# A hybrid decoder step in float32 on one Trainium2 core: sixteen places for the samples' value weights, new tokens' values over 128 rows, first modulation weights over eight places, one mixed block later

## What is computed

```
def modulated_prenorm(x, c, w_ada, b_ada, g_pre):
    mod = (jax.nn.silu(c) @ w_ada + b_ada)[:, None, :]
    shift, scale, gate = jnp.split(mod, 3, axis=-1)
    return rms_norm(x, g_pre) * (1 + scale) + shift, gate

def short_conv_mixer(h, conv_buf, w_in, w_conv, w_out):
    b_g, c_g, v, z = jnp.split(h @ w_in, 4, axis=-1)
    ...

def sample_latent_attention(q_lat, q_pe, ckv_new, kpe_new, cache_ckv, cache_kpe, page_table):
    ...
    p = jax.nn.softmax(jnp.concatenate([s_past, s_new], axis=-1), axis=-1).astype(ckv_new.dtype)
    return (jnp.einsum('bhqk,bkc->bqhc', p[..., :n_past], past_ckv)
            + jnp.einsum('bhqk,bkc->bqhc', p[..., n_past:], ckv_new))

def mla_output(o_lat, z, w_kv_up, w_out):
    b, t = o_lat.shape[:2]
    o = jnp.einsum('bthc,chv->bthv', o_lat, w_kv_up[..., QK_NOPE_DIM:]).reshape(b, t, D_ATTN)
    return (o * jax.nn.silu(z)) @ w_out
```

## Time and profile before

| | before |
|---|---|
| median of three runs | 2051.11 us |
| the profiled execution | 2052.14 us |
| its span, from the first to the last instruction | 2050.5 us |
| mean granted clock of TensorE, as a share of full speed | 0.99 |
| TensorE busy | 1978.3 us, 96% |
| VectorE busy | 1304.5 us, 64% |
| ScalarE busy | 805.1 us, 39% |
| GpSimd busy | 237.8 us, 12% |

### The profile page before, as it was taken

One profiled execution on the slowest core, in us unless ns is written; L12 is line 12 of the kernel. 1 busy time (PEld: TensorE's weight loads), 2 busy tenths in 40 slices (PEclk: granted clock), 3 DMA queues, 4 the chain that ended last, 5 costly groups with the idle time before them and its releaser, 6 DMA issues.

```text
span 2050.5 us, 42506 instructions
## 1 busy us (share of the span) xinstructions
PE 1978.3 (96%) x16316; PEld 1865.1 (91%) x16316; DVE 1304.5 (64%) x1992; ACT 805.1 (39%) x1222; POOL 237.8 (12%) x155
## 2 busy tenths in 40 slices
PE   4989999999999999999999999999999999999995
PEld 3889999999999999999999999999888876679995
DVE  4677777777777777797778820223443446659777
ACT  3243333333333333455455532223453434435443
POOL 1200000000000000000000333333122122201002
PEclk9999999999999999999999999999999999999997
DMA  9966655555555556744464222335313249752447
GB/s 392 406 214 220 206 202 190 190 197 205 205 206 199 198 194 207 258 142 135 140 249 175 84 83 83 103 124 170 93 52 101 82 156 340 232 162 91 141 158 268
DMA packets 128276, 371.79 MB, mean 181 GB/s; under 512 B 13170, under 2 KB 39666, under 8 KB 125874
## 3 DMA queue, kind: packets, MB, share of 16 engines
q1 hardware_dynamic: 123058, 353.64, 49.4%
q0 software_dynamic: 5120, 16.78, 2.7%
HBM read 343.76 MB, written 26.61 MB: 181 GB/s over the span
## 4 chain that ended last, share of the span: by engine, by line
PE 87%; DVE 5%; DMA 4%; ACT 1%; issue 1%; SPq 1%; POOL 0%; DVEq 0%; ACTq 0%
PE ps L879 31%; PE ps L883 15%; PE ps L767 8%; PE ps L774 4%; PE ps L833 3%; DMA s<-adastream 3%; PE ps L1335 3%; PE ps L1219 2%; PE ps L1361 2%; PE ps L1186 2%; PE ps L1201 2%; PE ps L1276 2%; PE ps L819 1%; PE ps L841 1%; PE ps L1159 1%; DMA w_raw<-wstream 1%
## 5 line engine op out<-in xcount | busy, mean ns | idle before, releaser
L715 POOL TENSOR_TENSOR w_split<-w_raw,w_split 128x1024 fp32r<-128x1024 f32 x78 | 191.8, 2459 | 1520.3 <-ACT w_split L1421 1520.3
L1483 ACT ACTIVATE w_split<-w_raw 128x1024 fp32r<-128x1024 f32 x176 | 186.3, 1058 | 332.7 <-PE ps L883 183.6
L1988 DVE TENSOR_TENSOR w_split<-w_raw,w_split 128x1024 fp32r<-128x1024 f32 x181 | 221.6, 1224 | 113.1 <-ACT w_split L1483 110.8
L879 PE MATMUL ps<-operand_hi,w_split 128*128 128x288 f32 x1056 | 283.4, 295 | 0.0
L879 PE MATMUL ps<-operand_lo,w_split 128*128 128x288 f32 x1056 | 283.3, 295 | 0.0
L879 PE MATMUL ps<-t_hi,w_split 128*128 128x288 f32 x960 | 262.9, 300 | 1.1 <-DVE c_u L2136 1.1
L879 PE MATMUL ps<-t_lo,w_split 128*128 128x288 f32 x960 | 258.0, 295 | 0.0
L879 PEld LDWEIGHTS ps<-operand_lo,w_split 128*128 128x128 f32 x1056 | 198.5, 188 | 0.0
L879 PEld LDWEIGHTS ps<-operand_hi,w_split 128*128 128x128 f32 x1056 | 198.4, 188 | 0.0
L1421 ACT ACTIVATE w_split<-w_raw 128x1024 fp32r<-128x1024 f32 (+1 forms) x90 | 93.6, 1040 | 258.3 <-PE ps L774 173.3
L879 PEld LDWEIGHTS ps<-t_hi,w_split 128*128 128x128 f32 x960 | 180.5, 188 | 10.5 <-issue 8.9
(11 more groups left out here) (375 smaller groups left out, 4076.6 us busy)
## 6 DMA issues: line engine op xcount, KB each, us to landing
w_raw<-wstream SPq DMA_DIRECT2D x183, 512.0 KB, 3.3
ada_ring<-adastream SPq DMA_DIRECT2D x114, 512.0 KB, 4.8
a<-wstream SPq DMA_DIRECT2D x88, 512.0 KB, 4.6
s<-wstream SPq DMA_DIRECT2D x44, 512.0 KB, 3.2
ada_first_ring<-adastream SPq DMA_DIRECT2D x32, 512.0 KB, 9.3
ada_third<-adastream SPq DMA_DIRECT2D x32, 512.0 KB, 6.5
x_residual<-x_in SPq DMA_DIRECT2D x8, 1152.0 KB, 8.7
tiles<-y_park SPq DMA_DIRECT2D x8, 1152.0 KB, 7.8
```

Source lines behind the costliest of these rows:

```text
L715: pool.tensor_tensor(WL[:, n.slot, 0:width], WR[:, n.slot, 0:width], WH[:, n.slot, 0:width].bitcast(F32), ALU.subtract).then_inc(w_lo_read ...
L879: pe.matmul(PS[:, bank, 0:HALF], WH[:, c.slot, k * P:(k + 1) * P], x(k), start=(first and k == 0 and x is hi), stop=False, skip_group_chec ...
L1483: act.activation(WH[:, c.slot, :], raw, ACT.Copy).then_inc(w_hi_ready, 1)
L1988: dve.tensor_tensor(WL[:, c.slot, :], raw, WH[:, c.slot, :].bitcast(F32), ALU.subtract).then_inc(w_lo_ready, 1)
```

## The change

It has four parts.

1. `FIRST8` becomes 64: all 64 chunks go round eight places. Chunks 62 and 63 use places 6 and 7 (`RA22` and `RS1`) instead of 0 and 1. The first product's loads into `RA21`, `RS1` and `RA22` wait for 64 used chunks instead of 56.
2. After block 5 VectorE makes two mixes instead of three and no low part; after block 6 it makes the third mix and both low parts.
3. `WV` becomes sixteen tensors in three free regions of the arena. SP issues ten loads when the last scores are done and six more when the values of seven batches are done (their region holds page latents until then). Four semaphores stand for four groups of four heads. The loop over heads on SP and on TensorE is written out.
4. `CKN` and `PTN` become 128 rows high. VectorE sets rows 64 to 127 to zero once, before the first batch. The three matmuls of the new tokens then run over 128 rows.

```
-FIRST8 = 56
+FIRST8 = 64
...
-        CKN = [at(f"new_latent_{n}", po + 4608 + i * R, [TS, R], F32R) for i, n in enumerate(("hi", "lo"))]
+        CKN = [at(f"new_latent_{n}", po + 4608 + i * R, [P, R], F32R) for i, n in enumerate(("hi", "lo"))]
...
-        WV = at("wv_ring", xo + 4608, [P, G, CT * VD])
...
-        PTN = [at(f"probs_t_new_{n}", o, [TS, P], F32R) for n, o in (("hi", po + 10880), ("lo", ro + NPG * P))]
+        PTN = [at(f"probs_t_new_{n}", o, [P, P], F32R) for n, o in (("hi", po + 10880), ("lo", ro + NPG * P))]
...
+        WV_AT = [*(xo + 4608 + i * R for i in range(6)), *(ao + i * R for i in range(4)), *(po + 5760 + i * R for i in range(6))]
+        WV = [at(f"wv{h}", o, [P, CT * VD]) for h, o in enumerate(WV_AT)]
...
             sp.wait_ge(sqk_done, NB * 3)
-            for s in range(G):
-                load_wv(s, s)
-            with sp.Fori(1, H // G) as i:
-                for s in range(G):
-                    sp.wait_ge(so_done, i * G + (s + 1 - G))
-                    load_wv(i * G + s, s)
+            for h in range(H):
+                if WV_AT[h] == po + 5760:
+                    sp.wait_ge(spv_done, NB - 1)
+                sp.dma_start(WV[h][:, :], wv_in[h, :, :]).then_inc(wv_landed[h // G], 16)
...
-            with pe.Fori(0, H // G) as i:
-                for s in range(G):
-
-                    pe.wait_ge(wv_landed[s], i * 16 + 16)
-                    pe.wait_ge(so_evac, i * G + (s + 1 - G + SO_BEGUN))
...
+            for h in range(H):
+                pe.wait_ge(wv_landed[h // G], 16 * G)
+                pe.wait_ge(so_evac, h + 1 - G + SO_BEGUN)
+                for k in range(CT):
+                    last = pe.matmul(PS[:, 4 + h % G, 0:P].rearrange("p (b t) -> p b t", b=NB), WV[h][:, k * VD:(k + 1) * VD],
+                                     QLAT[:, k, :, h // 2 * (2 * NS):(h // 2 + 1) * (2 * NS)],
+                                     start=(k == 0), stop=(k == CT - 1))
+                last.then_inc(so_done, 1)
...
                 if i == 5:
-                    mix_rest(0)
+                    mix_rest(0, False)
+                if i == 6:
+                    mix((1, 0), (1, 0), (1, 1), 0, HK // 2)
                     mixed_lo(0, 0, 0, 1, 3, 0)
-                if i == 6:
                     mixed_lo(1, 1, 1, 2, 4, 0)
...
             sample_new(0, 0, 0)
+            for t in (*CKN, *PTN):
+                dve.memset(t[TS:P, :].bitcast(F32), 0.0)
             step(dve.memset(PRN[:, :], 0.0))
```

More of the change, by code:

```diff
@@ L389, in build @@
             sem(n) for n in ("str_done", "spt_v", "spt_a", "spv_done", "ols_ready", "olt_done", "olt_evac"))
-        wv_landed = [sem(f"wv_landed{i}") for i in range(G)]
+        wv_landed = [sem(f"wv_landed{i}") for i in range(H // G)]
         so_done, so_evac = sem("so_done"), sem("so_evac")
@@ L661, in _ @@
                     load_keys(i * 2 + (2 + odd), odd, (sqk_done, i * 6 + (1 + 3 * odd)))
-            def load_wv(h, s):
-                sp.dma_start(WV[:, s, :], wv_in[bass.ds(h, 1), :, :].rearrange("a p n -> p (a n)")).then_inc(wv_landed[s], 16)
             sp.wait_ge(sqk_done, NB * 3)
-            for s in range(G):
-                load_wv(s, s)
-            with sp.Fori(1, H // G) as i:
-                for s in range(G):
-                    sp.wait_ge(so_done, i * G + (s + 1 - G))
-                    load_wv(i * G + s, s)
+            for h in range(H):
+                if WV_AT[h] == po + 5760:
+                    sp.wait_ge(spv_done, NB - 1)
+                sp.dma_start(WV[h][:, :], wv_in[h, :, :]).then_inc(wv_landed[h // G], 16)
             sp.wait_ge(olt_evac, NB + BEGUN)
@@ L2594, in new_latents @@
                 dve.wait_ge(new_done, 1)
-                step(dve.tensor_copy(CKN[0][:, :], PS[0:TS, 7, :]))
-                dve.tensor_tensor(CKN[1][:, :], PS[0:TS, 7, :], CKN[0][:, :].bitcast(F32), ALU.subtract).then_inc(new_evac, 1)
+                step(dve.tensor_copy(CKN[0][0:TS, :], PS[0:TS, 7, :]))
+                dve.tensor_tensor(CKN[1][0:TS, :], PS[0:TS, 7, :], CKN[0][0:TS, :].bitcast(F32), ALU.subtract).then_inc(new_evac, 1)
             def sample_probs(b, first):
@@ L2610, in sample_probs @@
                 dve.tensor_scalar(used, used, 0.0, None, ALU.mult)
-                dve.tensor_copy(PTN[0][:, :], PS[0:TS, 6, 0:P]).then_inc(spt_v, 1)
+                dve.tensor_copy(PTN[0][0:TS, :], PS[0:TS, 6, 0:P]).then_inc(spt_v, 1)
                 dve.wait_ge(spt_v, b * 2 + 1)
-                dve.tensor_tensor(PTN[1][:, :], PS[0:TS, 6, 0:P], PTN[0][:, :].bitcast(F32), ALU.subtract).then_inc(spt_v, 1)
+                dve.tensor_tensor(PTN[1][0:TS, :], PS[0:TS, 6, 0:P], PTN[0][0:TS, :].bitcast(F32), ALU.subtract).then_inc(spt_v, 1)
             def latents_low(b, odd, pages):
```

## The result

The kernel after takes 2040.28 us in the median of five runs (2039.78 to 2041.72); in the same session the kernel before took 2051.11 us (2049.88 to 2052.14, five runs). The ratio is 0.9946, 95% interval [0.9935, 0.9958]: 10.8 us less, where 10.2 were forecast. The profiled execution after took 2039.78 us with a span of 2038.1, 12.4 us less than the span before. That is more than the medians differ by: the profiled execution of before was the slowest of its five, that of after the fastest.

What follows compares the result with a forecast made beforehand. TensorE, busy for 96% of the span, was taken as the bound, with waits and half-clock stretches to remove. Terms 5.4 + 2.6 + 2.2 = 10.2 us gave 2040.9 for the median, 2041.9 for the profiled execution; range 2038 to 2046.

Steps and rivals of the forecast that it cites:

- The first stage: Last modulation blocks up to the first product: eight places and the later mix together save 5.4 us, bounds 3.6 and 6.7.
- the landing: Block 7's chunks 62 and 63 arrive at about 106.3 and 107.6, the weight chunk behind them at about 108.9.
- the margin of 1.3 us for chunk 63: Block 7: chunk 63 was to land 1.3 us before TensorE needs it, so no wait for it.
- The mixed block: Blocks 5 and 6: moving VectorE's third mix and low part later gains 0.35 us and costs nothing, with 0.6 us cover.
- the 1.93 us: Block 7: time VectorE's chain is held by GpSimd's pass over the last weight chunk, kept in the forecast.
- the bound's 1.3: Block 7: 1.3 us more gained if GpSimd's pass falls beside VectorE's chain; as a rival, chance 0.10, 2039.6.
- bounded it at 1.8 us: First stage: loss if the new 1.3 us wait lowers the clock, 17 matmuls at 0.24 instead of 0.134 us.
- the rival in which the new wait lowers the clock: Before block 7's last tiles: the new 1.3 us wait starts a half-clock stretch; slower, 2058.5 at 40 us, chance 0.03.
- The prediction's four microseconds at half clock: First stage, kernel before: after the 3.16 us wait for chunk 62 the granted clock is 0.50 for four microseconds.
- Sixteen places: Value heads: all weights in place save 2.3 us, the loop's set-up another 0.3; 2.6 us, bounds 1.0 and 3.5.
- 128 rows: New tokens' values: avoiding the change to 64 rows and back saves 0.27 us, eight times, 2.2 us; bounds 0 and 2.4.
- The rival that rows don't matter: New tokens' matmuls: the extra 0.27 us belongs to the change of operands, not of rows; 2043.1, chance 0.08.

Runs made afterwards that it cites:

- e1: Kernel before with only the sixty-four chunks over eight places; 2046.90 us, ratio 0.9981.
- e2: Kernel before with both first-stage edits, eight places and the later third mix and low parts; 2047.67 us, ratio 0.9981.
- e11: Kernel before with only the third mix and the low parts it feeds moved behind block 6; 2051.08 us, ratio 0.9994.
- e5: Kernel after with GpSimd's last pass of the first stage cut to 8 of 1024 columns, the rest left out; 2038.26 us, ratio 0.9936.
- e6: Kernel after with the first stage's last weight chunk loaded one block earlier, ahead of block 7's modulation chunks; 2040.60 us, ratio 0.9946.
- e10: Kernel after with GpSimd's last pass of the first stage waiting until VectorE has made all of block 7's operands; 2043.17 us, ratio 0.9954.
- e9: Kernel after with GpSimd's last pass of the first stage made in four passes of 256 columns instead of one of 1024; 2040.94 us, ratio 0.9943.
- e3: Kernel before with only the sixteen places for the value weights, loops on SP and TensorE as in the change; 2047.54 us, ratio 0.9983.
- e4: Kernel before with only the new tokens' values over 128 rows, with the four memsets; 2049.27 us, ratio 0.9987.
- e7: Kernel before with the heads' loops on SP and TensorE written out and the ring of four places kept; 2050.29 us, ratio 0.9993.
- e8: Kernel after with the samples' rotary scores over 128 rows too, zeros in the lower ones; 2040.89 us, ratio 0.9949.
- e12: Kernel after with VectorE instead of GpSimd making the low parts of the first stage's last weight chunk; 2039.25 us, ratio 0.9936.

## Why the prediction held, step by step

**The first stage, 5.4 us forecast.** Right in its mechanism, 0.9 us too large: 4.5 us in the traces, 3.9 by the ratios of e1 and e2 alike. The term that was mis-sized is the landing: chunks 62 and 63 "land at about 106.3 and 107.6, and the weight chunk behind them at about 108.9". By bytes this was right: at 108.6 only 0.1 MB was left, a quarter of a microsecond at 400 GB/s. But the transfers didn't keep that pace to the end. Their share is 0.99 from 107 to 108 us, 0.53 in the next and 0.10 in the one after, which is little more than one of the 16 engines; the last packets run until 110.0, and ScalarE began with the weight chunk 0.6 us behind them, at 110.64. TensorE got chunk 63 at 109.32. Both are 1.7 us behind the forecast, and the margin of 1.3 us for chunk 63 was none. The Trainium skill (DMA: Bandwidth & Descriptors, Anatomy of one DMA — SWDGE (gpsimd) path) gives each transfer a fixed cost of about 2 us beside its bytes, most of it behind the last byte. It states that for the transfers that GpSimd issues; these are SP's. The size is about that of the 1.7 us here, but the trace does not agree on where it lies: 0.6 us is behind the last packet, and the rest is the slow tail of the packets. The chain of transfers says it in one row (kernel after, chain that ended last: start, duration):
```profile
99.19 10.13 DMA s<-adastream
109.32 0.04 issue
109.36 0.65 PE ps L829 x16
```
So the turn came at 110.14 instead of 109.6, the held instruction took 2.72 instead of 2.48 us, and TensorE began 0.1 us behind the end of VectorE's chain (118.00), for which nothing was kept. These 0.54, 0.24 and 0.1 make the 0.9.

**The mixed block, 0.35 us of it.** Wrong as a gain: nothing (e2 against e1, e11), because the late chunk 63 absorbs it. That it costs nothing is right; the moved work ends at 108.9 as worked out.

**GpSimd's pass.** The choice to keep the 1.93 us was right, and e5 prices it at 1.4 us of start time, close to the bound's 1.3. The traces show it again and again: 2.72 for 0.55 after, and in e6 and e10 an addition of 2.16 and 2.03 us to passes of VectorE. The rule of the Trainium skill (SBUF — State Buffer, Who interferes with whom), that such instructions exclude each other and the second blocks until the first has ended, agrees with all of them; e9 adds that the next one can then be blocked by the next.

**The clock.** The forecast kept 0 for it in the first stage and bounded it at 1.8 us. All five profiled runs that keep the wait for chunk 62 (before, e3, e4, e7, e11; it is 2.5 to 3.4 us) show a granted clock between 0.50 and 0.82 in the 3 us from 112.1, and e10, with its wait of 2.96 us for GpSimd, shows 0.50 behind it (12 matmuls in 3 us instead of 24). In none of the other eight, where TensorE waits at most 1.5 us in one piece, does it fall there. So the rival in which the new wait lowers the clock fell for a wait of this size, and e10 shows that it wasn't idle: twice as long a wait brought it about. The prediction's four microseconds at half clock were read from one stretch and are too few: before, the clock is 0.50 from 111.5 to 118.2, nearly 7 us, and as long in e4; in e3, e7, e11 and e10 it is 3 to 4 us.

Little of what the eight places save is this clock, since VectorE's chain hides it: TensorE has to wait for block 7's operands anyway. From VectorE's turn to the first product it is 14.6 us before and 14.2 to 14.5 in the four other runs with the low clock; it is 14.4 after and 14.2 in e1, at full clock. Ahead of the turn the low clock takes 0.4 us: from the start of chunk 62 to the turn it is 2.5 us before, and 2.1 in e3, where the clock falls later. In e10 nothing hides it, and the last 48 matmuls take 7.8 us (119.88 to 127.70) instead of 6.5.

At the start of the heads it is not bound to one part: 0.50 before, 0.55 in e3 and 0.66 in e11, and 1.00 in the other eleven, with the ring and with the sixteen places, and with much the same waits of 0.8 to 1.2 us ahead of it. What decides it there stays open. It is why the two profiled executions differ by more than the medians: of the 4.2 us at the heads 2.6 are the places (e3, nearly the same clock); the other 1.6 is this stretch, as e3 and the kernel after, both with sixteen places, show (15.9 and 14.3 us).

**Sixteen places, 2.6 us.** Right, and a little small: the forecast had 2.3 in the stage and 0.3 for the loop's set-up ahead of it; measured are 2.6 at nearly the same half clock (3.0 to 3.3 at full clock) and 0.4. The loads were the pace and the four banks weren't, as forecast. Missing from the sum: output pair 1. I had noted that its five loads now leave before the heads (1814.31) and given it no value. In all eight profiled runs with sixteen places the wait there is 0.30 to 0.33 us; in the six with the ring it is 0.3, 0.3, 0.7, 1.2, 1.3 and 2.0, in the mean 1.0. So the 0.9 us of the table are what this pair of runs had, and 0.7 is nearer to what can be counted on. That the earlier loads bring this was not tried by itself.

**128 rows, 2.2 us.** Right: 2.1 in e4. The 2.5 between the two traces hold 0.4 that is the straight code's, ahead of the first head. The rival that rows don't matter fell. So did the plain lesson that 64 rows are bad: e8.

**The parts add up.** 3.9 (e2), 3.5 (e3) and 2.7 (e4) make 10.1 us against 11.1 by the ratio of the kernel after, within the intervals, which are about 1.8 us either way for each part and 2.4 for the whole. The forecast for the median, 2040.9 to 2041, came close partly because errors cancelled: 0.9 too much in the first stage, nearly 1 too little behind the heads.

## What to carry to other kernels

A wait of TensorE for a transfer is cured where its place in the ring comes free, not where the wait stands; but work out when the reader starts, not when the bytes would be through at full rate. When GpSimd and VectorE share a stage, count what GpSimd's pass takes from VectorE's chain: here 1.22 us on VectorE itself was cheaper than 2.39 us on GpSimd beside it. Before filling up 64-row matmuls to 128 rows, look whether neighbours use opposite halves: alone they cost a change of rows, in pairs they overlap.

## What the runs showed of the hardware that I had not expected

- Matmuls over rows 0 to 63 and 64 to 127 overlap: four entries of 384 columns (two float32 matmuls) take 0.84 us, change of rows included, and four over 128 rows 1.29 us (e8). The Trainium skill (TensorEngine Tiling (Array Packing), Key Properties) says that tiles work independently; the trace agrees.
- VectorE and GpSimd take turns at the grain of single instructions: four GpSimd pieces of 0.75 us hold four VectorE instructions for 1.98 us in all (e9), among them two of only 64 columns. GpSimd is slowed as well: 3.01 and 3.52 us (e9, e10) for a pass of 2.39.
- The queue of 512 KB transfers didn't end at full rate: behind 107.9 us the share of the engines falls from 1.0, the last 0.1 MB take from 108.6 to 110.0, and ScalarE starts on it at 110.64. It is much the same in seven other profiled runs (e1, e2, e5, e8, e9, e10, e12): the last packets end between 109.9 and 110.4, and ScalarE starts between 110.6 and 110.9.
- In the first stage a wait of TensorE of 2.5 to 3.4 us went with 3 to 4 us at 1.2 GHz in four profiled runs and nearly 7 us in two, and waits of up to 1.5 us with none in eight. Where no other wait hid it, the low clock cost 1.4 us (e10); behind the wait for chunk 62 it cost 0.4 to 0.8 us.
